# Three attention stages of a transformer kernel, with their opening operations in another order on the queues

## What is computed

```
# block 1 (stage 0 "moba", stage 1 "conv")
h = rms_norm(x) * (1 + scale1) + shift1
q, k, v, p, g_attn, g_pool = split(h @ w_in)          # 8 heads of 64
q, k = rms_norm per head;  logits = q k^T / 8 + bias(distance), causal;  attn = softmax(logits) v
pool = (trailing means of p over 2, 4, 8, 16 tokens - p) @ pool_w * pool_scale
x += gate1 * ((sigmoid(g_attn) * (attn @ w_a) + sigmoid(g_pool) * (pool @ w_p)) @ w_out)
x += gate2 * gated feed-forward with a causal 3-tap convolution
# block 2, two layers: ffn, mixer, ffn (stages 2 to 7)
swa: 16 heads, 4 key/value heads, window 128, bias, a sink per head in the softmax
fox: 16 heads, logits + F_q - F_k with F = cumsum(log_sigmoid(h @ w_f + b_f))
every norm is modulated: shift, scale, gate = silu(c) @ ada_w + ada_b, one set per stage
```

## Time and profile before

| | |
|---|---|
| median of 3 runs | 1499.24 us (1498.57 to 1499.58) |
| the profiled execution | 1496.46 us, span 1494.7 us, mean granted clock 0.982 |
| TensorE (PE) busy | 1408.8 us, 94% |
| weight loads (PEld) | 1165.3 us, 78% |
| VectorE (DVE) | 1085.8 us, 73% |
| ScalarE (ACT) | 732.8 us, 49% |
| GpSimd (POOL) | 140.3 us, 9% |
| moved by DMA | 333.63 MB, mean 223 GB/s |

### The profile page before, as it was taken

How to read it: one execution, slowest core, us unless ns; L and a number is a source line. 1 busy time by engine, 2 the same in 40 slices (tenths; PEclk the granted TensorE clock), 3 DMA queues, 4 the chain that set the end, 5 groups by cost and what they waited for, 6 DMA issues and landing times.

```text
span 1494.7 us, 18521 instructions
## 1 busy us (share of the span) xinstructions
PE 1408.8 (94%) x7262; PEld 1165.3 (78%) x7262; DVE 1085.8 (73%) x1523; ACT 732.8 (49%) x1036; POOL 140.3 (9%) x199
## 2 busy tenths in 40 slices
PE   2799898999989999988999999999999899999998
PEld 1578888999968888765678887788887676788886
DVE  5857887998988998747478778788877446466444
ACT  3454446444564334667553445643337557554332
POOL 1100100111001221000011110011110100000000
PEclk9899999999999999998999999999999989999999
DMA  9775756877959998440378886688963631475552
GB/s 351 252 221 178 259 180 208 277 266 241 314 161 347 343 355 303 161 167 4 102 242 309 302 294 242 219 302 294 304 235 113 199 113 57 141 253 176 184 183 76
DMA packets 189289, 333.63 MB, mean 223 GB/s; under 512 B 8850, under 2 KB 132478, under 8 KB 188180
## 3 DMA queue, kind: packets, MB, share of 16 engines
q1 hardware_dynamic: 161392, 236.02, 46.9%
q0 software_dynamic: 27232, 96.21, 18.9%
q10 hardware_dynamic: 580, 0.23, 0.1%
HBM read 331.27 MB, written 1.15 MB: 222 GB/s over the span
## 4 chain that ended last, share of the span: by engine, by line
PE 77%; DVE 10%; ACT 5%; DMA 4%; issue 3%; SPq 0%; ACTq 0%; POOL 0%; DVEq 0%; POOLq 0%
PE bank L1473 10%; PE bank L1475 10%; PE bank L1474 10%; PE bank L1436 8%; PE bank L1438 7%; PE bank L1437 7%; DVE lo L968 4%; PE bank L1368 3%; PE bank L1369 3%; PE bank L1370 3%; DMA ada<-in_ada_w 2%; DVE ada_sum L926 2%; PE bank L1601 2%; PE bank L1603 2%; PE bank L1602 2%
## 5 line engine op out<-in xcount | busy, mean ns | idle before, releaser
L968 DVE TENSOR_TENSOR lo<-raw,hi 128x2048 fp32r<-128x2048 f32 x215 | 490.9, 2286 | 83.5 <-ACT hi L535 82.7
L535 ACT ACTIVATE hi<-raw 128x2048 fp32r<-128x2048 f32 x215 | 405.8, 1910 | 31.4 <-DMA raw<-in_w_out 21.1
L1473 PE MATMUL bank<-hi,h_hi 128*128 128x512 f32 x704 | 278.1, 395 | 3.6 <-DVE lo L968 1.9
L1475 PE MATMUL bank<-hi,h_lo 128*128 128x512 f32 x704 | 274.6, 390 | 0.0
L1474 PE MATMUL bank<-lo,h_hi 128*128 128x512 f32 x704 | 274.1, 389 | 0.0
L1436 PE MATMUL bank<-hi,o_hi 128*128 128x512 f32 x504 | 203.7, 404 | 11.6 <-DVE lo L968 9.5
L1438 PE MATMUL bank<-hi,o_lo 128*128 128x512 f32 x504 | 197.3, 391 | 0.0
L1437 PE MATMUL bank<-lo,o_hi 128*128 128x512 f32 x504 | 196.5, 390 | 0.0
L647 ACT ACTIVATE KT<-bank 128x256 f32<-128x256 f32 x88 | 33.8, 384 | 311.9 <-PE bank L1475 311.9
L1473 PEld LDWEIGHTS bank<-hi,h_hi 128*128 128x128 f32 x704 | 132.2, 188 | 33.3 <-DVE lo L968 3.8
L1475 PEld LDWEIGHTS bank<-hi,h_lo 128*128 128x128 f32 x704 | 132.1, 188 | 28.1
(11 more groups left out here) (213 smaller groups left out, 2012.6 us busy)
## 6 DMA issues: line engine op xcount, KB each, us to landing
raw<-in_ffn_w SPq DMA_DIRECT2D x176, 512.0 KB, 5.3
ada<-in_ada_w POOLq DMA_DIRECT2D x100, 512.0 KB, 5.7
raw<-in_ffn_w SPq DMA_DIRECT2D x44, 1024.0 KB, 6.5
V<-in_ada_w POOLq DMA_DIRECT2D x76, 512.0 KB, 5.6
raw<-in_w_up SPq DMA_DIRECT2D x22, 1024.0 KB, 5.8
raw<-in_w_in SPq DMA_DIRECT2D x16, 1024.0 KB, 6.9
raw<-in_fox_w_in SPq DMA_DIRECT2D x12, 1024.0 KB, 5.3
raw<-in_w_down SPq DMA_DIRECT2D x11, 1024.0 KB, 6.2
```

The source lines that it names most:

```text
L535: nc.scalar.activation(hi[:, n % NS, :], raw[:, n % NS, :], ACT.Copy).then_inc(hi_ready, 1)
L968: nc.vector.tensor_tensor(lo[:, n % NS, :], raw[:, n % NS, :], hi[:, n % NS, :].bitcast(F32), ALU.subtract).then_inc(lo_ready, 1)
L1473: mm(bank[:, :], xk_hi, wh[:, i, :], start=k == 0, stop=False, skip_group_check=True)
L1475: ins = mm(bank[:, :], xk_lo, wh[:, i, :], start=False, stop=k == KD - 1, skip_group_check=True)
```

## The change

All operations stay but three of the unused `busy` matmuls (step 2 of swa) and one square root in swa, which takes two blocks' sums in one instruction. The rest is order:

- Prologue: unit 1's halves come between the two modulated tiles, on ScalarE and VectorE.
- moba: three ada pieces stand behind the norms in the opening instead of ahead of them, five in the attention's odd steps; the chunks' sums, columns and gates are placed at other units. TensorE's order of blocks is the same.
- swa: the first block's second tile is split by the first turns; the third block's second tile goes behind the logits wholly (3, 3 and 2 rows in steps 0 to 2), the late blocks are turned in steps 5 and 6 instead of 2 and 5.
- fox: the forget gates' product comes ahead of block (0,1), their chain on ScalarE and VectorE ahead of norm 2; rows behind the logits are eight a step in steps 0 to 5, all behind the logits of their step, instead of seven, the first seven ahead of the logits.

The tables, and the new helper:

```diff
-ROWS_FROM = {"swa": 12, "fox": 16}
-ROWS_STEP = {"swa": 2, "fox": 7}
+ROWS_FROM = {"swa": 8, "fox": 16}
+ROWS_STEP = {"swa": (3, 3, 2), "fox": (8,) * 6}
...
-        for u0 in (2, 3, 4, 4, 5, 5, 6, 7, 8, 9, 10, 11, 12, 12, 13, 14, 14, 15, 16, 16, 17, 17, 18, 18):
+        for u0 in (2, 7, 8, 9, 10, 11, 12, 12, 13, 14, 15, 16, 16, 17, 18, 18):
             PIECES_AT[w0 + u0] = PIECES_AT.get(w0 + u0, 0) + 1
-        SUMS_AT.update({w0 + u: 1 for u in (7, 9, 13, 17, 19, 22)})
-        COLS_AT.update({w0 + u: 1 for u in (8, 10, 14, 18, 20, 23)})
-        GATES_AT[w0 + 15], GATES_AT[w0 + 21] = (s0, 0), (s0, 1)
+        SUMS_AT.update({w0 + u: 1 for u in (7, 9, 11, 14, 18, 20)})
+        COLS_AT.update({w0 + u: 1 for u in (8, 10, 12, 15, 19, 21)})
+        GATES_AT[w0 + 16], GATES_AT[w0 + 22] = (s0, 0), (s0, 1)
...
+            def block_roots(s, e):
+                act.wait_ge(bsum_done, N0[s] + e + 2)
+                nc.scalar.activation(hstd[:, :, :], hstd[:, :, :], ACT.Sqrt, bias=eps[:, 0:1],
+                                     scale=1.0 / HD).then_inc(bstd_ready, 2)
```

ScalarE, prologue:

```diff
             modulated(0, 0)
+            split_to(1)
             modulated(0, 1)
-            split_to(1)
```

ScalarE, swa:

```diff
                     gate_copy(s, 1)
+                    block_evict(s, 0)
                     block_square(s, 2)
+                    block_evict(s, 1)
                     block_root(s, 2)
                     block_values(s, 1)
-                    block_evict(s, 0)
                     split_through(s, 5)
-                    block_evict(s, 1)
+                    block_evict(s, 2)
                     block_square(s, 3)
                     block_root(s, 3)
-                    block_evict(s, 2)
                     block_evict(s, 3)
+                    split_through(s, 6)
                     block_square(s, 4)
-                    split_through(s, 6)
                     for t in range(HEADS[kind] + 3):
                         attention_step(s, t)
-                        if t == 0:
-                            block_root(s, 4)
-                        elif t == 2:
-                            block_evict(s, 4)
+                        if t == 2:
                             block_square(s, 5)
                         elif t == 3:
-                            block_root(s, 5)
-                        elif t == 5:
-                            block_evict(s, 5)
+                            block_roots(s, 4)
+                        elif t in (5, 6):
+                            block_evict(s, t - 1)
```

ScalarE, fox:

```diff
                     gate_copy(s, 1)
-                    block_square(s, 2)
-                    block_root(s, 2)
-                    block_evict(s, 0)
-                    split_through(s, 5)
...
+                    block_evict(s, 0)
+                    block_square(s, 2)
+                    split_through(s, 5)
+                    block_root(s, 2)
                     block_evict(s, 1)
                     block_square(s, 3)
                     block_root(s, 3)
+                    block_evict(s, 2)
                     split_through(s, 6)
-                    block_evict(s, 2)
+                    block_evict(s, 3)
                     block_values(s, 0)
                     split_through(s, 7)
-                    block_evict(s, 3)
```

VectorE, moba:

```diff
                     block_norm(s, 0)
+                    pieces(1)
                     split_through(s, 4)
                     block_sums(s, 1)
                     block_norm(s, 1)
+                    pieces(1)
                     split_through(s, 5)
...
                     split_through(s, 6)
+                    pieces(1)
                     for t in range(HEADS[kind] + 3):
                         attention_step(s, t)
+                        pieces(int(t in (1, 3, 5, 7, 9)))
```

VectorE, swa:

```diff
                     block_sums(s, 1)
+                    block_norm(s, 1)
                     split_through(s, 4)
-                    block_norm(s, 1)
...
                         if t in (0, 3):
                             block_sums(s, 4 + t // 3)
-                            block_norm(s, 4 + t // 3)
+                        elif t == 4:
+                            block_norm(s, 4)
+                            block_norm(s, 5)
```

TensorE, steps:

```diff
-                        step_rows(s, 0)
                         pe.wait_ge(bk_ready, N0[s] + 4)
                     attention_step(s, t)
                     if t in turns:
                         turn_block(s, 4 + turns.index(t))
-                    if t:
-                        step_rows(s, t)
-                    if kind == "swa" and 2 <= t < 9:
+                    step_rows(s, t)
+                    if kind == "swa" and 3 <= t < 9:
                         busy(3)
```

TensorE, swa:

```diff
+                        block_rows(s, 0, 1, 0, 4)
                         turn_block(s, 0)
+                        block_rows(s, 0, 1, 4, KD)
                         turn_block(s, 1)
+                        block_rows(s, 1, 1, 0, 6)
                         turn_block(s, 2)
+                        block_rows(s, 1, 1, 6, KD)
+                        block_rows(s, 2, 0, 0, 5)
                         turn_block(s, 3)
+                        block_rows(s, 2, 0, 5, KD)
+                        steps(s, (5, 6))
```

TensorE, fox, behind the forget gates' product:

```diff
+                    block_rows(s, 0, 1, 0, 4)
+                    turn_block(s, 0)
+                    block_rows(s, 0, 1, 4, KD)
                     block_rows(s, 1, 1, 0, 4)
+                    turn_block(s, 1)
                     block_rows(s, 1, 1, 4, KD)
                     turn_block(s, 2)
+                    block_rows(s, 2, 0, 0, 6)
                     turn_block(s, 3)
+                    block_rows(s, 2, 0, 6, KD)
+                    block_rows(s, 2, 1, 0, KD)
                     steps(s, (3, 4, 5, 6))
```

More of the change, by code:

```diff
@@ L1317, in _ @@
                     block_sums(s, 1)
-                    split_through(s, 4)
                     block_norm(s, 1)
-                    block_sums(s, 2)
-                    split_through(s, 5)
-                    block_norm(s, 2)
                     dve.wait_ge(fl_done, 1)
@@ L1327, in _ @@
                                                    op0=ALU.mult, op1=ALU.min).then_inc(fz_ready, 1)
+                    split_through(s, 4)
                     dve.wait_ge(f_ln, 1)
@@ L1334, in _ @@
                                                  ALU.mult, ALU.add).then_inc(cum_done, 1)
-                    block_sums(s, 3)
-                    block_norm(s, 3)
                     dve.wait_ge(cum_done, 1)
@@ L1346, in _ @@
                                             ALU.mult).then_inc(nft_ready, 1)
+                    block_sums(s, 2)
+                    block_norm(s, 2)
+                    split_through(s, 5)
+                    block_sums(s, 3)
+                    block_norm(s, 3)
                     split_through(s, 7)
@@ L1620, in step_rows @@
                 kind = KINDS[s]
-                first = ROWS_FROM[kind] + ROWS_STEP[kind] * t
-                for r in range(first, min(first + ROWS_STEP[kind], 2 * KD * (len(BLOCKS[kind]) - 2))):
+                first = ROWS_FROM[kind] + sum(ROWS_STEP[kind][:t])
+                for r in range(first, first + sum(ROWS_STEP[kind][t:t + 1])):
                     n = r // KD
@@ L1847, in _ @@
                     gate_rows(s, 1)
-                    block_rows(s, 0, 1, 0, KD)
                     if kind == "swa":
-                        block_rows(s, 1, 1, 0, 4)
+                        block_rows(s, 0, 1, 0, 4)
                         turn_block(s, 0)
-                        block_rows(s, 1, 1, 4, KD)
+                        block_rows(s, 0, 1, 4, KD)
                         turn_block(s, 1)
-                        block_rows(s, 2, 0, 0, 6)
+                        block_rows(s, 1, 1, 0, 6)
                         turn_block(s, 2)
-                        block_rows(s, 2, 0, 6, KD)
-                        block_rows(s, 2, 1, 0, 4)
+                        block_rows(s, 1, 1, 6, KD)
+                        block_rows(s, 2, 0, 0, 5)
                         turn_block(s, 3)
-                        steps(s, (2, 5))
+                        block_rows(s, 2, 0, 5, KD)
+                        steps(s, (5, 6))
                         continue
@@ L1868, in _ @@
                     ins.then_inc(fl_done, 1)
+                    block_rows(s, 0, 1, 0, 4)
+                    turn_block(s, 0)
+                    block_rows(s, 0, 1, 4, KD)
                     block_rows(s, 1, 1, 0, 4)
-                    turn_block(s, 0)
+                    turn_block(s, 1)
                     block_rows(s, 1, 1, 4, KD)
-                    turn_block(s, 1)
-                    block_rows(s, 2, 0, 0, KD)
                     turn_block(s, 2)
-                    block_rows(s, 2, 1, 0, 4)
+                    block_rows(s, 2, 0, 0, 6)
                     turn_block(s, 3)
-                    block_rows(s, 2, 1, 4, KD)
+                    block_rows(s, 2, 0, 6, KD)
+                    block_rows(s, 2, 1, 0, KD)
```

## The result

The changed kernel takes 1485.72 us (median of 4 runs, 1484.69 to 1486.51) against 1498.9 us (4 runs, 1498.11 to 1499.58): ratio 0.9909, 95% interval 0.9894 to 0.9924. The gain is 13.2 us, half of the 26.3 us forecast, and 0.3 us inside the end of the range at 1486. The profiled execution took 1485.89 us, 1484.1 of it span, so between the two traces the gain is 10.6 us: the kernel before had been profiled in an execution 2.4 us under the median of its four runs, the changed one 0.2 above.

What follows compares the result with a forecast made beforehand. TensorE is busy 94% of the span, so time can come only from its waits and low-clock stretches. Gains of 10.0 + 3.5 + 6.3 + 6.5 = 26.3 us take the median from 1499.24 to 1472.9 us; range 1466 to 1486.

Steps and rivals of the forecast that it cites:

- Moba's opening: Before moba's logits: waits for unit 1 and the norms go, logits start at 80.0 instead of 90.02, 10.0 us gained.
- The rest of moba: Moba's attention and pool split: new ada pieces cost nothing, the 3.34 us wait shrinks; 3.5 us gained, bounds 0 and 5.2.
- Swa: Swa attention: earlier logits and one pair of table changes, less new waits; 6.3 us gained, bounds 3 and 7.4.
- Fox: Fox attention: forget rows no longer waited for, logits earlier, a new wait at head 8; 6.5 us gained, bounds 3 and 9.6.
- Its work is then 8.7 us a step, until step 6 has no rows left: Fox's steps after step 2: TensorE, 9.6 us ahead there, keeps 8.7 us a step until step 6.
- Part 3: The swa forecast, 6.3 us; it has unit 5's data issued at 644.1, landing 5.2 us later, wanted at 656.
- The wait at head 8: Fox, behind step 6 without rows: TensorE waits for ScalarE's last eviction, uncovered by matmuls, 3.1 us lost.
- Hand-overs eat part of it: Rival, all stages: thin margins and new waits leave only the lower bounds, 13.3 us gained, 1485.9 us; chance 0.23.
- Order frees nothing: Rival: TensorE meets the same producers, waits shift by one block, only unit 1 is gained; 1495.2 us; chance 0.06.
- Slower: Rival, swa's steps and half of fox's: a wait drops the clock to 0.51 and it stays; 1504 us at 32 us; chance 0.03.
- the sign that the prediction itself had set as proof against it: Anywhere in the kernel: the forecast is wrong if the clock of 0.5 lasts past 16 us.
- part 4: The fox forecast, 6.5 us: 9.6 us ahead at step 2, less a 3.1 us wait at head 8.

Runs made afterwards that it cites:

- the tiles' swap: The kernel before with only unit 1's halves put between the two tiles of the modulated input, on ScalarE and VectorE: 1495.28 us, ratio 0.9985.
- rows by sevens: The changed kernel with fox's 48 late row products dealt 7, 7, 7, 7, 7, 7, 6 to steps 0 to 6 instead of eight to steps 0 to 5: 1468.96 us.

## Why the prediction was right and wrong

**Moba's opening, right.** 80.0 forecast, 79.50 measured, 10.0 and 10.5 us; the one wait left, 0.6 forecast, is 0.49. The value at the upper end was the right one to take, and both halves of the change were needed for it: with the tiles' swap alone a wait of 1.96 us appeared at the first norm.

**The rest of moba, right in size, not in its parts.** 3.5 forecast, 4.3 at the end of the attention, 2.9 behind the next stage. The pool split wait went entirely, not to 1.5 less; the new wait of 2.30 us at unit 13 was not seen, though the text had counted the column reduction ahead of that low half. It was set only against the pool split, not against unit 13 itself.

**Swa, right.** 6.3 forecast, 7.1 measured (7.2 alone). The table changes came as one pair, the wait in step 5 is 3.39 us (3.3 forecast), the one at head 8 only 1.30 (2.5 forecast). On the table load the rows of this trace agree with the earlier one: the load takes 1.28 us and the root starts 0.02 us behind its end (659.06 and 660.36). The 1380 ns drain of the Trainium skill, "ScalarE: Activation LUTs", section What ACT_TABLE_LOAD costs, shows in neither kernel; ahead of the load the line is unbroken too (the copy before it ends at 659.05).

**Fox, wrong, and by more than its bounds.** Up to step 4 every point came: logits at 1160.68, which with the 20.56 us gained earlier is 1181.24 on the old scale (1181.3 forecast), no wait for the forget rows, step 2 at 1197.4 on that scale (1197.0), the third turn's wait 0.77 us (1.65 forecast). The failing step is the sentence "Its work is then 8.7 us a step, until step 6 has no rows left". It priced eight rows by their matmuls alone. Eight instead of seven also pull the last four rows that read a new unit from step 5 into step 4, and their low half is made in step 4: 5.2 us of wait and some 2 of slow matmuls, 7.1 us together by the span of the run that makes it a step earlier. Part 3 had checked unit 5's arrival; for units 9 to 11 nobody asked.
The second step is the bound. The wait at head 8 was forecast at 3.1 us and measured at 3.18; that the clock falls behind it stood only in the lower bound, 3.5 us under the value, of which 1 us was for ScalarE, so 2.5 us for the clock. It cost 6.4 us, shown by filling the wait and leaving head 8 where it was. So fox's lower end, 3, should have been 0 or a little less (6.5 less 6.4), even without the low half. In all fox came out 16.2 us under its forecast: 8.2 up to head 8 (it came to fox 20.6 us ahead of the kernel before and to head 8 only 18.9 us ahead), and 8.0 behind it, where the steps to their end take 50.5 us instead of 42.5.

**The rival that came true did so by accident.** *Hand-overs eat part of it* gave 1485.9 us and 1485.72 were measured, but it had every stage short; in truth moba and swa came in full and fox was 16 us off. That the time fell inside the stated range is luck for the same reason. *Order frees nothing* is refuted by 83.76 and 79.50 for the logits. *Slower* named the right mechanism (a wait drops the clock and it stays); its price, 0.8 to 1 us for each us of work, was too high here, since the four steps behind head 8 took 19.5 us where rows by sevens has 12.9. The argument against it, that no low stretch had lasted longer than 16 us, was drawn from a kernel in which row products or filling matmuls stood within 8.2 us behind each of those waits (in fox from 1197.65 on, with full clock from 1203.3). In the changed kernel it lasted 22 us, the sign that the prediction itself had set as proof against it.

**The sum.** With rows by sevens the span is 1467.7, that is 27.0 us under that of the kernel before, where 26.3 had been summed: the rest of the working holds, though the nearness of the two sums is partly chance. Before fox 19.4 us were gained (19.8 forecast). In fox it was 9.4 up to head 8, the 9.6 of part 4 without its wait of 3.1, and 1.6 were lost again to the clock at the first output products. The step from the profiled execution to the median added another 2.8 us that the changed kernel did not have; in later runs the kernel before scattered from 1493.95 to 1504.18.

## What to carry to other kernels

When work is dealt out again over the steps of a pipeline, write down for each step not only how much there is, but which operand the last of it reads and in which step that operand is made; one row more a step cost 16.8 us. Price a wait on TensorE also by what stands behind it: here four steps of short matmuls took 19.5 us instead of 12.9 behind a wait of 3.2, and eleven unused matmuls in the wait brought 6.3 us back. And work moved from ahead of one wait has to be followed to its new place: ask what hides it there before calling the wait removed.

## What was not expected of the hardware

A single wait of 3.18 us was followed by about 22 us at 1.2 GHz, although TensorE was busy for all 14.38 us of the first window by the trace (in which the ends of matmuls are modelled), in steps of short logits, turns and values; it came back with the twelve output products at 1245 to 1249. In swa, in the kernel with rows by sevens, the clock behind a wait of 3.38 us was 0.64 for 6.8 us (666.22 to 673.06) and then full, with three filling matmuls in each step; without them it was 0.57 over 24 us. The Trainium skill, "TensorE: Matmul & The Clock Gate", section Loop structure matters more than you think, says that the loop nest decides whether matmuls stay at full clock, and blames waits for data between them. The runs agree on the waits; what the nest does behind the wait weighed more here, 6.4 us against the 3.18 of the wait itself. They also show falls that no long wait explains: to 0.53 for 3.3 us behind waits of 0.21 and 0.56 us (rows by sevens, 1227.26), and for 3.3 us amid row products (swa without its filling, 1168.50).
